# Adding the experts' rows to the residual rows in memory, with ten expert places and other first loads, in a hybrid encoder layer

## The reference, cut to what matters

```python
h = h + parallel_mixer(rmsnorm(h, g_mix), w_in, ...)            # gated heads and neighbourhood attention
h = h + memory_cross_attention(rmsnorm(h, g_xattn), ...)
h = h + hierarchical_moe(rmsnorm(h, g_moe), w_rg, w_re, w_gate, w_up, w_down)
return rmsnorm(h, g_final)

def hierarchical_moe(hn, ...):                                   # top-1 of 4 groups, top-2 of its 8 experts
    gates = sum(one_hot(expert_id, 32) * weights)                # (tokens, 32), two nonzero in a row
    act = silu(xf @ w_gate[e]) * (xf @ w_up[e]) * gates[:, e]    # for all experts e, d_expert = 128
    out = sum_e act @ w_down[e]
```

## Time and profile before

| | us |
|---|---|
| median of 3 runs (1284.52 to 1288.79) | 1287.25 |
| the profiled execution's own time | 1285.98 |
| its span, first to last instruction | 1284.4 |
| PE busy in the span | 1155.7 (90%) |
| DVE busy | 668.8 (52%) |
| ACT busy | 469.1 (37%) |
| POOL busy | 253.4 (20%) |

### The profile page before, as it was taken

One profiled execution on the slowest core, in us unless ns is written; L12 is line 12 of the kernel. 1 busy time (PEld: TensorE's weight loads), 2 busy tenths in 40 slices (PEclk: granted clock), 3 DMA queues, 4 the chain that ended last, 5 costly groups with the idle time before them and its releaser, 6 DMA issues.

```text
span 1284.4 us, 18164 instructions
## 1 busy us (share of the span) xinstructions
PE 1155.7 (90%) x6249; PEld 957.8 (75%) x6249; DVE 668.8 (52%) x1276; ACT 469.1 (37%) x970; POOL 253.4 (20%) x375
## 2 busy tenths in 40 slices
PE   4999999999998999999999999999977999999900
PEld 3888888878887888888889788778766787777600
DVE  5332332311116888433366664754567987763267
ACT  5222222200005666211224333544224666663222
POOL 1222222100002222001101000000022433333244
PEclk9999999999999999999999999999987999999955
DMA  8555353663138312442222001001556999999186
GB/s 288 134 186 162 114 160 115 233 164 70 33 85 215 83 23 75 144 157 88 82 64 89 1 1 66 18 17 49 214 213 204 383 362 352 380 361 340 41 335 256
DMA packets 108742, 204.19 MB, mean 159 GB/s; under 512 B 39550, under 2 KB 51838, under 8 KB 108670
## 3 DMA queue, kind: packets, MB, share of 16 engines
q1 hardware_dynamic: 84974, 146.62, 35.0%
q0 software_dynamic: 17280, 44.07, 10.0%
q10 hardware_dynamic: 6416, 12.59, 3.0%
HBM read 163.06 MB, written 55.10 MB: 170 GB/s over the span
## 4 chain that ended last, share of the span: by engine, by line
PE 77%; DMA 7%; DVE 4%; SPq 3%; ACT 3%; issue 2%; POOL 2%; POOLq 0%; DVEq 0%; ACTq 0%
PE bank L516 17%; PE bank L518 16%; PE bank L517 16%; PE bank L2108 4%; PE bank L1907 4%; DMA at<-in_w_exp_down 4%; PE bank L2036 3%; PE bank L1887 3%; PE bank L2074 2%; PE bank L2094 2%; PE bank L1896 2%; PE bank L1833 2%; PE bank L2045 2%; DVE at L1759 1%; PE bank L1970 1%
## 5 line engine op out<-in xcount | busy, mean ns | idle before, releaser
L516 PE MATMUL bank<-at,at 128*128 128x512 f32 (+1 forms) x1208 | 448.2, 371 | 6.5 <-DVE at L511 4.1
L518 PE MATMUL bank<-at,at 128*128 128x512 f32 (+1 forms) x1208 | 437.5, 362 | 0.0
L517 PE MATMUL bank<-at,at 128*128 128x512 f32 (+1 forms) x1208 | 436.6, 361 | 0.0
L516 PEld LDWEIGHTS bank<-at,at 128*128 128x128 f32 x1208 | 228.7, 189 | 42.5 <-DVE at L511 4.6
L518 PEld LDWEIGHTS bank<-at,at 128*128 128x128 f32 x1208 | 228.3, 189 | 35.7
L517 PEld LDWEIGHTS bank<-at,at 128*128 128x128 f32 x1208 | 228.8, 189 | 32.7
L511 DVE TENSOR_TENSOR at<-at,at 128x1024 fp32r<-128x1024 f32 (+3 forms) x160 | 183.8, 1160 | 113.5 <-ACT at L506 106.9
L506 ACT ACTIVATE at<-at 128x1024 fp32r<-128x1024 f32 (+3 forms) x160 | 153.9, 992 | 168.0 <-DVE at L1402 48.5
L809 POOL TENSOR_TENSOR at<-at 128x1 f32<-128x1 f32 x88 | 26.9, 306 | 523.4 <-ACT at L1144 282.3
L2108 PE MATMUL bank<-at,at 128*128 128x512 f32 x156 | 74.2, 597 | 3.3 <-ACT at L1218 3.0
L922 POOL DMA_INDIRECT y_tok<-at,at x39 | 39.9, 1023 | 151.7 <-DVE at L1721 131.4
(11 more groups left out here) (191 smaller groups left out, 1352.1 us busy)
## 6 DMA issues: line engine op xcount, KB each, us to landing
at<-in_w_exp_gate SPq DMA_DIRECT2D x39, 512.0 KB
at<-in_w_exp_up SPq DMA_DIRECT2D x39, 512.0 KB
at<-in_w_exp_down SPq DMA_DIRECT2D x39, 512.0 KB
at<-y_tok SPq DMA_DIRECT2D x24, 512.0 KB, 9.9
xT_hi_all<-at POOLq DMA_DIRECT2D x12, 512.0 KB, 3.9
xT_lo_all<-at POOLq DMA_DIRECT2D x12, 512.0 KB, 5.7
at<-xT_hi_all SPq DMA_DIRECT2D x3, 2048.0 KB, 11.4
at<-xT_lo_all SPq DMA_DIRECT2D x3, 2048.0 KB, 13.5
```

Source lines behind the costliest of these rows:

```text
L516: nc.tensor.matmul(out, w_hi, x_hi, start=(k == 0), stop=False)
L517: nc.tensor.matmul(out, w_lo, x_hi, start=False, stop=False)
L518: last = nc.tensor.matmul(out, w_hi, x_lo, start=False, stop=(k == len(terms) - 1))
```

## The change

Four things change. (1) The gate is applied to the activation of a slot (`gated`), from a table `gate_slot` made like the slot table by products on PE. (2) The residual rows `H` are stored to a tensor `h_sum` in memory as their tiles become final, and each scatter adds its block to `h_sum`; scatter(b) waits until scatter(b-1) has landed. The tail loads the sums, one load of 512 KB a tile, squares, scales and stores them. (3) The freed place of `H` holds four more experts: ten places, experts 3 to 7 loaded earlier. The overflow blocks use six of the ten places. (4) The first loads are in halves and in another order, the first two tiles of `x` among them on SP's queue; `g_mix` is loaded as rows and turned on PE; the three first projections start on half of their weights.

```diff
+W_RING = 10
+OVER_SLOTS = (2, 6, 8, 9, 0, 1)
-        y_tok = dram("y_tok", [2 * T, D])
+        h_sum = dram("h_sum", [T, D])
-        slots_kb = [48, 60, 108, 84, 72, 96]
+        slots_kb = [48, 60, 108, 0, 12, 24, 84, 36, 72, 96]
...
-            sp.dma_start(w_uvv[1][:, 0:KT // 2], w_in[:, 0:KT // 2, HALF:2 * HALF]).then_inc(w_v_here, 16)
-            sp.dma_start(w_uvv[1][:, KT // 2:], w_in[:, KT // 2:, HALF:2 * HALF]).then_inc(w_in_here[1], 16)
-            sp.dma_start(w_uvv[0], w_in[:, :, 0:HALF]).then_inc(w_in_here[0], 16)
-            sp.dma_start(w_uvv[2], w_in[:, :, 4 * HALF:5 * HALF]).then_inc(w_in_here[2], 16)
+            sp.dma_start(x_in[0], a["x_prompt"][0][0:P]).then_inc(rows_here[0], 16)
+            load_w_in(1, 1)
+            load_w_in(0, 0)
+            sp.dma_start(x_in[1], a["x_prompt"][0][P:2 * P]).then_inc(rows_here[1], 16)
+            load_w_in(2, 4)
...
+            def keep_rows(t):
+                sp.wait_ge(mm_evac, n_groups["xo", t, 1] + 1)
+                sp.dma_start(h_sum[t * P:(t + 1) * P], H[:, t]).then_inc(h_moved, 16)
+            for t in range(2 * TPC):
+                keep_rows(t)
             sp.wait_ge(mm_done, n_groups["o", NCH - 1, XH - 1] + 1)
             for e in range(3):
-                load_gate_up(e, e)
-                load_down(e, e)
+                load_expert(e)
+            sp.wait_ge(h_moved, 16 * 2 * TPC)
+            sp.wait_ge(n_ready, n_norms["moe", 2] + 1)
+            load_expert(3)
+            sp.wait_ge(n_ready, n_norms["moe", 5] + 1)
+            load_expert(4)
+            keep_rows(8)
+            sp.wait_ge(h_moved, 16 * 9)
+            sp.wait_ge(n_ready, n_norms["moe", 8] + 1)
+            load_expert(5)
+            for t in (9, 10, 11):
+                keep_rows(t)
             sp.wait_ge(mm_done, n_groups["xo", NT - 1, 1] + 1)
-            load_gate_up(3, 3)
-            load_down(3, 3)
+            load_expert(6)
+            sp.wait_ge(h_moved, 16 * NT)
+            sp.wait_ge(n_ready, n_norms["moe", 11] + 1)
+            load_expert(7)
             sp.wait_ge(mm_done, len(groups))
...
-            for e in (4, 5):
-                load_gate_up(e, e)
-                load_down(e, e)
-            for e in range(RING, NE):
-                sp.wait_ge(gu_done, e - RING + 1)
+            load_expert(8)
+            load_expert(9)
+            for e in range(W_RING, NE):
+                sp.wait_ge(gu_done, e - W_RING + 1)
...
-            def load_y(t):
-                for k in range(2):
-                    sp.dma_start(y_g[t][k], y_tok[k * T + t * P:k * T + (t + 1) * P]).then_inc(yg_here[t % AHEAD], 16)
+            def load_sum(t):
+                sp.dma_start(H[:, t], h_sum[t * P:(t + 1) * P]).then_inc(sum_here[t % AHEAD], 16)
...
             def scatter(b):
                 pool.wait_ge(y_evac_s, b + 1)
                 pool.wait_ge(y_evac_v, b + 1)
-                pool.indirect_dma_start(out=y_tok, out_offset=bass.IndirectOffsetOnAxis(ap=slot_dst[:, b:b + 1], axis=0), in_=y_st[b % 2],
-                                        in_offset=None, bounds_check=2 * T - 1, oob_is_err=False).then_inc(y_sent[b % 2], 16)
+                if b > 0:
+                    pool.wait_ge(y_sent[(b - 1) % 2], 16 * ((b - 1) // 2 + 1))
+                pool.indirect_dma_start(out=h_sum, out_offset=bass.IndirectOffsetOnAxis(ap=slot_src[:, b:b + 1], axis=0), in_=y_st[b % 2],
+                                        in_offset=None, bounds_check=T - 1, oob_is_err=False, compute_op=ALU.add).then_inc(y_sent[b % 2], 16)
...
-            step(nc.vector.tensor_scalar(second[:, 0:NE], bank[7][:, 0:NE], float(-T), float(T), ALU.is_ge, ALU.mult))
-            nc.vector.scalar_tensor_tensor(slot_src[:, 0:NE], bank[7][:, 0:NE], float(2 * T), second[:, 0:NE], ALU.add, ALU.subtract).then_inc(table_ready, 1)
-            nc.vector.tensor_scalar(slot_dst[:, 0:NE], bank[7][:, 0:NE], float(2 * T), None, ALU.add).then_inc(table_ready, 1)
+            nc.vector.tensor_scalar(slot_src[:, 0:NE], bank[7][:, 0:NE], float(T), None, ALU.add).then_inc(table_ready, 1)
...
+            def place_gates(g):
+                gates_of = gate[:, :, TG * g:TG * (g + 1)].unsqueeze(3).to_broadcast([P, 2, TG, NE])
+                nc.vector.tensor_tensor(in_gate[g], one[g], gates_of, ALU.mult).then_inc(slot_ready, 1)
...
-                nc.vector.tensor_tensor(e_out[j], silu_g[j], bank[2 + j][:, FE:2 * FE], ALU.mult).then_inc(e_act, 1)
+                one_gate = gate_slot[:, b:b + 1] if isinstance(b, int) else gate_slot[:, bass.ds(b, 1)]
+                nc.vector.scalar_tensor_tensor(e_out[j], silu_g[j], one_gate, bank[2 + j][:, FE:2 * FE], ALU.mult, ALU.mult).then_inc(e_act, 1)
...
+            gate_values()
+            for g in range(NT // TG):
+                place_gates(g)
             for h in range(2):
                 split_expert(0, h)
+            count_overflow()
+            dve.wait_ge(slots_done, 4)
+            step(nc.vector.tensor_copy(gate_slot[:, 0:NE], bank[7][:, NE:2 * NE]))
             keep_experts(2)
-            gate_values()
-            count_overflow()
             split_xg(0)
...
-                dve.wait_ge(yg_here[t % AHEAD], 32 * (t // AHEAD + 1))
-                    nc.vector.scalar_tensor_tensor(H[:, t], y_g[t][k], gate[:, k, t:t + 1], H[:, t], ALU.mult, ALU.add).then_inc(f_add, 1)
+                nc.vector.scalar_tensor_tensor(out_rows[t], H[:, t], rs[:, 16 + t:17 + t], gf_row, ALU.mult, ALU.mult).then_inc(f_out, 1)
...
+            def turn_gating_weights():
+                pe.wait_ge(sgu_w_gv_here, 32)
+                for n in range(2):
+                    for h in range(4 * n, 4 * n + 4):
+                        turned = nc.tensor.transpose(bank[6 + n][:, (h % 4) * P:(h % 4 + 1) * P], sgu_nat[:, h], ident)
+                    turned.then_inc(g_sgu_t, 1)
+            def project_first(out, n, done):
+                for k in range(KT):
+                    if n == 2 and k == KT // 2:
+                        turn_gating_weights()
+                    if k % (KT // 2) == 0:
+                        pe.wait_ge(lo_made, LO_W_IN[n, k // (KT // 2)] + 1)
...
+            for g in range(NT // TG):
+                pe.wait_ge(slot_ready, 9 + g + 1)
+                for k in range(2):
+                    for t in range(TG):
+                        last = nc.tensor.matmul(bank[7][:, NE:2 * NE], in_place[g][k][:, t].bitcast(F32), in_gate[g][:, k, t],
+                                                start=(g == 0 and k == 0 and t == 0), stop=(g == 2 and k == 1 and t == TG - 1))
```

More of the change, by code:

```diff
@@ L282, in hymba_encoder, with sum_count @@
         y_sent = pair("y_sent")
-        f_add, f_out = sem("f_add"), sem("f_out")
-        yg_here, out_sent = [sem(f"yg_here_{n}") for n in range(AHEAD)], sem("out_sent")
+        f_out = sem("f_out")
+        sum_here, out_sent = [*rows_here, *(sem(f"sum_here_{n}") for n in range(2, AHEAD))], sem("out_sent")
+        def sum_count(t):
+            return (16 + 16 * NT // 2 if t % AHEAD < 2 else 0) + 16 * (t // AHEAD + 1)
         TPC = CH // P
@@ L950, in square_x @@
             def square_x(i, j):
-                act.wait_ge(x_here[j], 16 * (i + 1))
-                first = is_first(i, j)
+                first = isinstance(i, int) and i == 0
+                if first:
+                    act.wait_ge(rows_here[j], 16)
+                else:
+                    act.wait_ge(x_here[j], 16 * i)
                 if not first:
-                    act.wait_ge(sgu_t, 2)
+                    act.wait_ge(g_sgu_t, 3)
+                if not is_first(i, j):
                     act.wait_ge(x_sq[1 - j], i + j)
@@ L1237, in _, with overflow @@
             evac_y(NE - 1, (NE - 1) % 2, (NE - 1) // 2)
-            def overflow(b, j, n, r, half):
+            def overflow(b, j, n, i, half):
                 silu(b, j)
@@ L1295, in tile_work @@
                 nxt = (i, 1) if j == 0 else (i + 1, 0)
-                if not last:
+                if not last and not is_first(i, j):
                     scale_x(*nxt)
@@ L1538, in keep_experts @@
                 experts = iota_e.unsqueeze(1).unsqueeze(1).to_broadcast([P, 2, TG, NE])
[L1539 removed]
+                step(nc.vector.tensor_tensor(one_rank, one[g], experts, ALU.mult))
                 step(nc.vector.tensor_reduce(first_of[:, :, TG * g:TG * (g + 1)], one_rank, AX, ALU.add))
@@ L1794, in project_first_v @@
-                last.then_inc(v_done, 1)
+                halves = [range(KT // 2 * half, KT // 2 * (half + 1)) for half in range(2)]
+                for half, ks in enumerate(halves):
+                    pe.wait_ge(hi_made, max(HI_W_IN[1, half], HI_X0) + 1)
+                    for k in ks:
+                        nc.tensor.matmul(bank[2][:], x_hi[0][:, k], w_uvv_hi[1][:, k], start=(k == 0), stop=False)
+                    pe.wait_ge(lo_made, LO_X0 + 1)
+                    for k in ks:
```

(3 more changed lines are left out.)

328 lines of the change are left out of this document (173 added, 155 removed).

## The result

The changed kernel takes 1328.62 us (median of 4 runs, 1327.96 to 1330.27); the kernel before, beside it, 1285.88 us (4 runs, 1283.29 to 1288.79). The ratio is 1.033, 95% interval 1.031 to 1.036: slower by 43 us. The forecast was 1280, range 1248 to 1328, so the time lies just outside. The profiled execution's span went from 1284.4 to 1326.4 us, +42.0.

What follows compares the result with a forecast made beforehand. PE bound most of the kernel, with DMA also near full in the experts and PE empty in the tail. 1285.98 - 8.5 + 0.5 + 33.8 - 8 - 25 = 1278.8, plus 1.3: 1280 us, range 1248 to 1328.

Steps and rivals of the forecast that it cites:

- Start: Kernel start: x ahead of the weights and split loads bring the first gating product earlier, 8.5 us gained (5 to 10).
- Before the experts: Stretch before the first expert block: extra stores and loads fit, 24 gate-table products added; +0.5 us (-1 to +4).
- The clock that should rise earlier: PE before the first block: working instead of idling, its half clock should rise earlier; part of the +0.5 us.
- Experts: Expert blocks 0 to 31: waiting adding scatters set 7.0 us a block instead of 5.91, +33.8 us.
- The 7.0: Expert blocks: an adding scatter's issue to landing, taken as 7.0 us a block, with 5.9 to 10 open.
- a free add: Expert scatters: had the add been free, 6.1 us a block and a time of 1255 us.
- Overflow: Scatter 31 to 38: PE already up to two blocks ahead, so 39 us instead of 47.3, -8 us.
- Tail: Kernel end: half the loads, fewer bytes and no DVE operations of 1.282 us; -25 us (-19 to -29).
- A (hidden): Experts: adding scatters land within a block of PE and stay hidden; 1250 us, chance 0.18 together with D.
- B (the DMA's rate): Experts: the DMA's rate, not the chain, is the bound; +14.7 us, 1269 us, chance 0.10.
- C: Experts: reading the old row delays packets, landings take 8 us or more; 1310 us at 8.0, chance 0.32.
- D: Early expert weights are not loaded earlier, held by SP's waits; costs 4 us only in A, chance 0.18 with A.

Runs made afterwards that it cites:

- the start alone: The kernel before the change with only the new first loads and their splits; experts, scatters and tail as before: 1280.55 us, ratio 0.995.

## Why the prediction was wrong

**Start: right.** 8.5 forecast, 8.2 measured at the gating product and 7.1 at gather 0 where the start stands alone.

**Before the experts: wrong, +0.5 forecast, +6.7 measured.** The step was "eight like them took 1.89 us, so 24 take 5.7". Products of plain float32 are two records each, so 24 took 10.45 us. With one record each they took 5.30, and the table cost 1.3 us. The mechanism was right, the count was off by a factor of two. The clock that should rise earlier didn't: the first block's transposes begin at 971.36 us in both kernels, and in both the granted clock is 0.50 up to 977 us and 1.00 from 980 on, though PE now works through the gate table where it stood idle. The extra stores and loads cost little: gather 0 of the changed kernel is 0.6 us behind the one with the start alone, inside the spread.

**Experts: the failed step, +33.8 forecast, +67.7 measured.** The step was "Serial, each scatter's issue to landing is the least time of a block". That the serial chain decides was right, and the landing, forecast at 7.0, is 7.2. But a serial wait costs landing plus hand-over, and the sum had put the 0.88 us of hand-over at nothing: 27 of the 34 us that were missed. The other 0.2 us a block are 6.

The 7.0 was right by luck. I had built it of 5.1 us for a lone adding scatter and 1.9 for the weights beside it. The runs show 6.2 without weights, and 0.7 to 1.3 for the weights. The 0.4 us in the 1.9 for engines that carry more than the mean was tested by no run. The add's 0.9 us is near the engines' time (0.9 to 1.1 a scatter) and too little for the chain, where the add costs 1.3 us a block (2.8 in block 0): I had put the same number in both places. A smaller slip: with a free add the prediction's own steps give 1252 us (1280 less 31 x 0.9), not 1255.

**Overflow: -8 forecast, -5.1 measured.** That PE rules here was right. Its block took 7.3 us and not 7.0, and PE was only one block ahead of scatter 31, not two: the down product of block 32 ended at 1238.9, 3.3 us before that scatter started, and the next one began at 1244.07.

**Tail: -25 forecast, -20.9 measured.** Right bounds, a rate of 371 instead of 403 GB/s, and the last landing 2 us longer.

**The rivals.** A (hidden) fell: with the wait, even a plain scatter costs 30 us. B (the DMA's rate) is false for the changed kernel, whose DMA share from scatter 0 to 31 is 0.86 in the table of stretches (0.98 only from 1000 to 1060 us), but it is what binds once the wait is removed. C said 8 us a block and more. The block is 8.08 us, but for another reason than C gave: the landing stayed under 8 in the mean. Its 1310 us for 8.0 fell short by the gate table, the overflow and the tail, which all erred to one side. D fell: the early weights did come early (from 904 to 953.4 us the DMA share is 0.96 at 367 GB/s, against 0.56 at 214), and it made no difference that shows in the serial kernel.

What stays open: why block 0's adding scatter lands 2.8 us later when its second read takes about 0.9 us of the engines' mean time and its instruction 0.6 us more, and why it is 1.3 us a block over the chain. The trace doesn't look inside a transfer.

## What to carry to other kernels

A chain of DMAs, each waiting for the one before, costs landing plus hand-over per link; take both from a row where one DMA really waits for another, since overlapped DMAs show neither. Before you serialise for the sake of shared rows, look for an order in which neighbours share none: here that was worth 45 us. And count a product's passes by its records in the trace, for the exact type that it will have.

## What the runs showed of the hardware that I had not expected

- An adding scatter's instruction takes 1.59 us on POOL, a plain one's 1.01; block 0's landing is 6.7 against 3.9 us, a nearly empty one's 4.5 against 2.6.
- The old rows read by an add don't appear among the bytes of the queue (43.03 against 43.02 MB), only in its share (12.7% against 10.2%). The 292 GB/s alone would have read as engines with room, at a share of 0.95.
- With two adding scatters in flight beside the weights each landed after 10.9 us, not 7.5, so that they came 6.3 us apart against 8.1 one at a time, where PE alone would have allowed 5.6.
- A 128x32 product of plain float32 is two records of 0.22 us each at half clock (48 in 10.45 us), a one-pass one is one (24 in 5.30 us).
